# All attentions in one common cycle of head groups, with later heads' projections as products in its first cycles

## The reference

```python
x = layer_norm(ALPHA * x + y, ln_g[i, 0], ln_b[i, 0])          # y: the mixer of layer i
x = layer_norm(ALPHA * x + memory_cross_attention(x, mem_k, mem_v, x_w_q[i], x_w_o[i]), ...)
x = layer_norm(ALPHA * x + conv_glu_ffn(x, f_w_up[i], ...), ...)
...
heads = jnp.concatenate([mix, mem_out], axis=1)                # second stack
h = h + merge_heads(heads) @ w_out[layer]
```

## Time and profile before

| | |
|---|---|
| median of 3 runs | 2282.67 us |
| the profiled execution | 2284.04 us |
| its span | 2282.7 us |
| PE busy | 2114.5 us (93%) |
| PEld busy | 1915.4 us (84%) |
| DVE busy | 1544.2 us (68%) |
| ACT busy | 1181.1 us (52%) |
| mean granted clock of PE | 0.964 |

### The profile page before, as it was taken

One profiled execution on the slowest core, in us unless ns is written; L12 is line 12 of the kernel. 1 busy time (PEld: TensorE's weight loads), 2 busy tenths in 40 slices (PEclk: granted clock), 3 DMA queues, 4 the chain that ended last, 5 costly groups with the idle time before them and its releaser, 6 DMA issues.

```text
span 2282.7 us, 34082 instructions
## 1 busy us (share of the span) xinstructions
PE 2114.5 (93%) x13749; PEld 1915.4 (84%) x13749; DVE 1544.2 (68%) x2655; ACT 1181.1 (52%) x2031; POOL 91.9 (4%) x160
## 2 busy tenths in 40 slices
PE   7979999888899989899989899998988999989998
PEld 7758899787799978789977678997967999878997
DVE  4674777786677776577777657777465776766776
ACT  4444455493355555445545435554444555465554
POOL 3000000000000010000000000001000000000000
PEclk9999999998999989999989999998988999999999
DMA  8414566455366554366643336665605665424662
GB/s 276 147 57 147 176 185 182 133 170 171 102 195 185 178 155 120 112 180 189 181 159 125 117 106 216 182 184 139 195 24 148 194 193 181 138 93 139 194 188 90
DMA packets 436205, 356.24 MB, mean 156 GB/s; under 512 B 15858, under 2 KB 381686, under 8 KB 436048
## 3 DMA queue, kind: packets, MB, share of 16 engines
q1 hardware_dynamic: 429296, 332.49, 48.3%
q0 software_dynamic: 6752, 21.57, 2.7%
HBM read 352.97 MB, written 1.05 MB: 155 GB/s over the span
## 4 chain that ended last, share of the span: by engine, by line
PE 80%; DVE 11%; ACT 5%; issue 2%; POOL 1%; DMA 1%; SPq 0%; DVEq 0%; ACTq 0%
PE psum L493 20%; PE psum L495 20%; PE psum L494 20%; PE psum L905 14%; PE psum L811 2%; PE psum L798 2%; DVE w_lo L1411 1%; DVE xt_lo L1426 1%; DVE x_tok L1772 1%; PE psum L768 1%; ACT e L1253 1%; DVE e L1678 1%; DMA tok<-in_mem_dram 1%; ACT w_hi L1023 1%; DVE n_tok L1750 1%
## 5 line engine op out<-in xcount | busy, mean ns | idle before, releaser
L1411 DVE TENSOR_TENSOR w_lo<-w_raw,w_hi 128x1024 fp32r<-128x1024 f32 x639 | 751.4, 1224 | 207.4 <-ACT w_hi L1023 205.5
L493 PE MATMUL psum<-xt_hi,w_hi 128*128 128x256 f32 x2744 | 792.5, 289 | 24.0 <-DVE w_lo L1411 15.5
L494 PE MATMUL psum<-xt_lo,w_hi 128*128 128x256 f32 x2744 | 789.8, 288 | 0.0
L495 PE MATMUL psum<-xt_hi,w_lo 128*128 128x256 f32 x2744 | 789.0, 288 | 0.0
L1023 ACT CAST w_hi<-w_raw 128x1024 fp32r<-128x1024 f32 x639 | 645.9, 1048 | 107.3 <-PE psum L495 77.9
L493 PEld LDWEIGHTS psum<-xt_hi,w_hi 128*128 128x128 f32 x2744 | 540.8, 197 | 33.6 <-DVE xt_lo L1426 11.7
L494 PEld LDWEIGHTS psum<-xt_lo,w_hi 128*128 128x128 f32 x2744 | 540.9, 197 | 4.4
L495 PEld LDWEIGHTS psum<-xt_hi,w_lo 128*128 128x128 f32 x2744 | 540.2, 197 | 0.0
L1841 DVE SCALAR_TENSOR_TENSOR qt<-psum,par,qt 128x255 f32<-128x255 f32 (+1 forms) x528 | 218.0, 475 | 165.5 <-ACT qt L1329 165.2
L493 PE MATMUL psum<-w_hi,xt_hi 128*128 128x512 f32 (+4 forms) x700 | 256.2, 366 | 12.4 <-DVE xt_lo L1426 11.8
L495 PE MATMUL psum<-w_hi,xt_lo 128*128 128x512 f32 (+4 forms) x700 | 253.3, 362 | 0.0
(11 more groups left out here) (215 smaller groups left out, 1917.6 us busy)
## 6 DMA issues: line engine op xcount, KB each, us to landing
w_raw<-in_f_w_up_dram SPq DMA_DIRECT2D x176, 512.0 KB, 5.1
w_raw<-in_f_w_down_dram SPq DMA_DIRECT2D x88, 512.0 KB, 5.1
w_raw<-in_w_up_dram SPq DMA_DIRECT2D x88, 512.0 KB, 5.1
w_raw<-in_w_down_dram SPq DMA_DIRECT2D x44, 512.0 KB, 5.1
w_raw<-in_x_w_q_dram SPq DMA_DIRECT2D x32, 512.0 KB, 4.7
w_raw<-in_x_w_o_dram SPq DMA_DIRECT2D x32, 512.0 KB, 4.8
w_raw<-in_a_w_qkv_dram SPq DMA_DIRECT2D x24, 512.0 KB, 4.5
w_raw<-in_w_in_fox_dram SPq DMA_DIRECT2D x20, 512.0 KB, 4.8
```

The lines of the kernel that those rows point to most:

```text
L493: self.eng.matmul(out, stat[0], mov[0], start=first, stop=False)
L494: self.eng.matmul(out, stat[0], mov[1], start=False, stop=False)
L495: return self.eng.matmul(out, stat[1], mov[0], start=False, stop=last)
L1411: self.up(self.eng.tensor_tensor(self.m.lo[:, s, :], self.m.raw[:, s, :], self.m.hi[:, s, :].bitcast(F32), ALU.subtract), "w_lo", u)
```

## The change

`attend(e, groups, fill, settle)` replaces every `attention`: one cycle for all kinds, run by all engines. A `Group` knows its heads, its kind and its banks: scores in banks 2 and 3 (the two heads of a group; in cross by turns), turned probabilities in 4 and 5, values' output in 6 and 7. Banks 0 and 1 are left for products in the first cycles. Mixer and memory groups of the second stack form one list of 8, without a stage between them.

```diff
+def attend(e, groups, fill, settle):
+    n = len(groups)
+    e.scores(groups[0])
+    for c in range(n + 3):
+        if c >= 3:
+            e.output(groups[c - 3])
+        if 2 <= c <= n:
+            e.values(groups[c - 2])
+        if c < n:
+            e.shift(groups[c])
+        if 1 <= c <= n:
+            e.normalise(groups[c - 1])
+        fill(e, c)
+        if c == n + 1:
+            e.values(groups[n - 1])
+        if c < n:
+            e.exponentials(groups[c])
+        settle(e, c)
+        if c + 1 < n:
+            e.scores(groups[c + 1])
+        if 1 <= c <= n:
+            e.transposes(groups[c - 1])
+            e.probabilities(groups[c - 1])
+    for j in range(KT // 2):
+        e.sum_unit(j)
```

`shift` is `maxima` under a new name. A call that an engine's class doesn't define does nothing there, so each engine's order follows from this list. `fill` issues projections, `settle` Scalar's copies of them:

```diff
+def sliding(e, j):          # fill: c 0, 1: query_half(c); c 2: turn_query_half.  settle: c 2: keep_query_half
+def latent(e):              # fill: c 0, 1: latent_keys(c + 2), latent_query(c + 2).  settle: their copies
+def cross(e, l):            # fill: c 0, 1: cross_query(c + 2).  settle: its copy
+def forgetting(e):          # fill: c 0, 1, 2: forgetting_tiles(c + 3).  settle: its copies
+def dilated(e):             # fill: c 0: late_queries; c 1: turn_late_queries, late_keys; c 2: turn_late_keys, memory_queries
...
+    def query_half(self, c):                          # Vector
+        self.units(2)
+        if c == 1:
+            self.wait_ge("turned", self.tag, "k", 2)
+            self.rotated_tokens("q1", (0, 1), BANK, 0)
...
+    def score_bank(self, i):
+        return 2 + (i if self.of.per == 2 else self.g % 2)
```

More of the change, by code:

```diff
@@ new lines @@
+    cross_start = cross_query = keep_cross_query = forgetting_start = forgetting_tiles = nothing
+    keep_forgetting_tiles = dilated_start = late_queries = turn_late_queries = keep_late_queries = nothing
+    late_keys = turn_late_keys = keep_late_keys = memory_queries = keep_memory_queries = nothing
+    scores = shift = exponentials = normalise = transposes = probabilities = values = output = nothing
+    sum_unit = out_finish = feed_forward = nothing
+def attend(e, groups, fill, settle):
[23 more added lines that the diff above has]
+        e.sum_unit(j)
@@ new lines, in cross_query, with scores @@
+            return
+        k = (None, 6, 0, 1)[j]
+        self.claim(k)
+        for a in range(2):
+            self.used(self.feature_out(m.pair(k)[:, a, :], self.take(KT, P)), "made", self.tag, "q", j)
+        self.free[k] = ("kept", self.tag, "q", j)
+    def scores(self, group):
+        scored, score, _, _ = self.ways[group.of]
+        mask = group.of.mask
+        scored(group.g)
+        for i, h in enumerate(group.heads):
+            k = group.score_bank(i)
+            self.claim(k)
+            for b in range(TB):
+                ins = score(h - group.first, b, self.m.psum[:, k, KEYS[mask][b]])
+            self.up(ins, "scored", self.tag, h)
+            self.free[k] = ("masked", self.tag, h) if mask else ("exps", self.tag, group.g)
@@ L1710, in attention @@
-        for g in range(a.groups + 2):
-            if g < a.groups:
-                maxima(g)
-            if g >= 3:
-                output(g - 3)
-            if 1 <= g <= a.groups:
-                normalise(g - 1)
-        output(a.groups - 1)
-    def memory_attention(self):
-        for j in range(MEMORY.tile0):
-            self.counts[("ready", (self.tag, "out"), j)] = self.counts[("ready", (self.mixer, "out"), j)]
-        self.attention(MEMORY)
-    def out_project(self, part):
-        self.units(KT // 2)
+        if self.e_read[s] is not None:
+            self.wait_ge(*self.e_read[s])
@@ new lines, in shift @@
+        if a.mask and not a.decay:
+            self.wait_ge("masked", self.tag, group.heads[-1])
+        else:
+            self.after(self.step(ins))
+        if a.sink:
+            self.after(self.step(self.eng.tensor_tensor(mx, mx, sink, ALU.max)))
+        ins = self.eng.tensor_scalar(nm, mx, -(1.0 if a.mask else a.scale), None, ALU.mult)
+        if a.sink:
+            self.after(self.step(ins))
+            ins = self.eng.tensor_tensor(m.small[:, s, 0:n], nm, sink, ALU.add)
+        self.up(ins, "shift", self.tag, group.g)
```

1000 lines of the change are left out of this document (558 added, 442 removed).

## The result

The changed kernel takes 2309.9 us (median of 4 runs, 2307.59 to 2312.72), the kernel before took 2282.59 us on the same chip; the ratio is 1.0119, 95% interval 1.0106 to 1.0131. The change makes the kernel 1.2% slower. The profiled run took 2307.59 us, the shortest of its four, so spans of single profiled executions show a little less than the medians do: 23.6 us against 27.3.

The account below looks back on a forecast made before the run. TensorE is busiest, but the steady sliding cycle is bound by a chain through transposes and VectorE. Sliding 11.2, cross 0.8, latent 3.8, second stack 5.2 and 5.5 sum to 26.5 us; 2282.7 + 26.5 = 2309 us, range 2284 to 2324.

Parts of the forecast that it names:

- Step (a), the loop: VectorE running `output` before `shift` closes a loop through exponentials, copies and `xt_hi`: sliding cycle 5.22 us against 4.10.
- rival 2: First cycles go as worked out, but `output` in front of `shift` costs nothing: +3.4 us, 2286 us; chance 0.14.
- Step (b), two banks: Two score banks instead of four: hidden for masked groups, 0 to 3.8 us per memory attention.
- tails: Ends of the second stack's attentions, with drain and bank waits: -0.4 us in layer 0, +1.5 in layer 1.
- Step (c), exposed copies: `values` directly after `transposes` leaves TensorE standing about 0.9 us each time; slack where VectorE sets the cycle.
- The logits: Forget logits first in second stack, layer 0, at low clock: 10.3 instead of 5.4 us; start +1.75 (bounds -3, +5).
- Rival 1: Neither new VectorE order nor exposed copies lengthen a cycle; fill hides all early waits: -23.7 us, 2259 us; chance 0.10.
- Rival 3, the clock: TensorE's clock falls too, in about half of the 20 longer cycles or at output projections: 12 us more, 2321; chance 0.16.

Follow-up runs that it names:

- experiment 3: The changed kernel with `values(c-2)` moved behind `scores(c+1)`, ahead of `transposes(c-1)`, and `output` still ahead of `shift`: 2328.9 us.
- experiment 1: The changed kernel with one order put back, `output(c-3)` behind `shift(c)` in the common cycle: 2274.6 us.
- experiment 6: The changed kernel with `output` behind `shift` and the later heads' projections ahead of the attention instead of in its first cycles: 2302.9 us.

## Why the prediction was right, step by step

The forecast was 2309 us, and 2309.9 was measured; its attentions were to cost 26.5 us, and their stages cost 26.9. Part of that agreement is luck, and the experiments show which.

- **Step (a), the loop: right in mechanism and place.** 5.22 us were worked out, 5.16 are there, with the pieces as forecast, and opening the loop alone takes 35 us away, closing it alone in the kernel before costs 25.7. The size over all attentions was too small: rival 2 left 23.1 us out of the sum for it, the kernel without the loop has 33.3 less in the attentions. Most of the gap is the second stack: I counted the mixer groups (3.9 and 3.8 us) and left the memory groups out, where the order goes on costing. Measured are 7.9 and 6.7. The sliding attentions had some 4.7 us each in the sum and cost 6.2 and 7.7, with five longer cycles instead of four and, in the second, a clock of 0.91. Cross went the other way, 1.2 counted and 0.8 measured, four times.
- **Step (b), two banks: right place, and priced too cheaply.** Hidden for masked groups, a wait in the memory groups; with the bounds of 0 to 3.8 each, the two cost 3.7 and 3.1 with the loop and 2.1 without. I had netted them into tails of -0.4 and +1.5. The Trainium skill's rule that I set beside it ("Perfetto Trace Analysis", Optimizing Tensor Performance: rotate through different banks) holds here for the second memory groups, whose bank is freed by ScalarE, at these prices. No run gave the masked groups their four banks back; but with two and without the loop the sliding cycle is at its old 4.10 us with no wait for a bank, so nothing was left to pay there.
- **Step (c), exposed copies: right, at less than the 0.9 us each that I took.** They are 0.56 to 0.68 us in the masked cycles with the loop, and slack: with the copies covered, experiment 3 has the same 5.15 us a cycle at full clock. In cross, 0.95 us an attention could be had by covering one of the four.
- **The logits: the clock was forecast (0.50 for 10.3 us), its price was not.** I took +1.75 us; their place is worth nothing, since the products behind them pay instead.
- **What is left without the loop: the gain was forecast too small.** The sum without the loop stood at +3.4 us (rival 2, 2286 us). The kernel of experiment 1 has a ratio of 0.9950, about 2271 us against the forecast's base, and its attention stages have -7.5 us against before. The misses are in dilated (forecast +1.7, measured -2.6), sliding (+0.9 each; -0.3 and -1.3) and forgetting (+1.3; -0.6); cross was right in sum (-4.0 and -4.4). That a better cover of the first cycles made them is my reading; experiment 6 prices the cover only against none at all. So 10 us too little for the loop and 11 too much for the rest of these stages cancelled. Rival 2 is therefore wrong in its condition (the order costs a lot), and its price was wrong as well.
- **Rival 1** asked for both (a) and (c) to cost nothing and had 2259 us; with (a) undone, the copies covered and the banks moved, 2267 is as far as it went.
- **Rival 3, the clock,** was there in part. The second sliding attention took 55.41 us, the first 53.92, with one code; the memory scores needed 3.44 instead of 1.99 us. The granted clock was 0.91 to 0.97 over the masked attentions and 1.00 over the cross ones, where the earlier trace rows had 0.93 to 1.00; without the loop it is 1.00 over all of them. These two rows come to some 3 us; 12 were priced. What the clock cost in all is not separated from the loop.
- The unforecast -3.3 us of the other stages are of the size by which equal code scatters.

## What to carry to other kernels

When a new order puts an operation ahead of another on an in-order engine, follow what the moved one waits for right round to itself: here a 0.42 us subtraction in front of the masking turned three parallel chains into one loop and cost 26 to 34 us of span, while the busy times of VectorE and ScalarE stayed within 1 us and TensorE's grew by 8 to 15 us, at a lower clock. Price such an order over all groups that run through it, not only over the steady ones, and with the other edits in place: two faults that delay the same chain cost more together. And a wait that shows on the busiest engine is worth removing only when it is on the loop; the same edit cost 18.6 us with the loop and gave 2.0 without it. When an order costs more than its dependencies explain, look at the granted clock of single cycles before giving the time to the order.

## What was unexpected of the hardware

The projections behind a norm ran at a granted clock of 1.00 over a stretch in one kernel and at 0.64 and 0.79 over the same stretch, same code, in another, 2.5 us apart. Unchanged stages together moved the span by up to 6 us from kernel to kernel, more than most single edits here were worth; the clock was followed only through this one stretch. In the loops, the length of a cycle went with the clock: in experiment 3 the granted clock went back and forth between its two levels, and a sliding cycle was 5.15 us at 1.00 and 6.6 to 6.8 us with a low stretch in it, where the value products took 1.56 instead of 0.88 us. The changed kernel, with the same 5.15 us cycle but three shorter pauses of TensorE, was at its low level for a shorter time (0.97 over its first sliding attention, 0.85 there).
